# HGRN's level work as instruction threads of its own, and three output-projection blocks beside the last RWKV step

## The reference, cut to what matters

```
# HGRN, each head, forward and backward in time; f = gate in (0,1)
bcum  = cumsum(log f)                       # within a chunk
S     = exp(total) * S + k * exp(total - bcum) @ v
o_t   = sum_{s<=t} (q_t . exp(bcum_t - bcum_s) . k_s) v_s + (q_t * exp(bcum_t)) @ S

# RWKV-7, then the projection of all mixers' outputs
state = state * d + (state @ a) b + v k     # per token
y     = group_norm(state @ r) * ln_w + ln_b + bonus, times g
x     = x + concat(out_a, out_b, out_m) @ w_out
```

## Time and profile before

| what | value |
|---|---|
| time of three runs | 3525.97, 3529.41, 3529.43 us (median 3529.41) |
| the profiled execution | 3524.7 us, of it span 3522.9 us |
| granted TensorE clock, mean | 0.979 of full |
| TensorE busy (PE) | 3341.1 us, 95% |
| VectorE, ScalarE, GpSimd busy | 1490.8, 1082.6, 395.9 us |

### The profile page before, as it was taken

How to read it: one execution, slowest core, us unless ns; L and a number is a source line. 1 busy time by engine, 2 the same in 40 slices (tenths; PEclk the granted TensorE clock), 3 DMA queues, 4 the chain that set the end, 5 groups by cost and what they waited for, 6 DMA issues and landing times. The chain is left out here.

```text
span 3522.9 us, 38396 instructions
## 1 busy us (share of the span) xinstructions
PE 3341.1 (95%) x16568; PEld 2582.1 (73%) x16568; DVE 1490.8 (42%) x2056; ACT 1082.6 (31%) x1619; POOL 395.9 (11%) x386
## 2 busy tenths in 40 slices
PE   6999999889899999999999989999998999999999
PEld 2466666666758888888877766788886888888887
DVE  6256624665444111113346442556543433333333
ACT  4243324334233111112135553233323322222211
POOL 1022202343212000000012000111211100000000
PEclk9999999999999999999999999899998999999999
DMA  5111110000042111112122010000003111110211
GB/s 234 41 60 61 72 39 24 13 13 24 1 153 75 48 48 48 48 36 91 46 72 83 36 37 18 8 1 1 1 1 150 54 48 48 48 48 30 96 44 71
DMA packets 35257, 182.33 MB, mean 52 GB/s; under 512 B 4261, under 2 KB 4261, under 8 KB 21648
## 3 DMA queue, kind: packets, MB, share of 16 engines
q1 hardware_dynamic: 22176, 133.18, 10.6%
q0 software_dynamic: 12912, 46.69, 3.4%
HBM read 161.89 MB, written 17.96 MB: 51 GB/s over the span
## 5 line engine op out<-in xcount | busy, mean ns | idle before, releaser
L537 PE MATMUL ps<-r,r 128*128 128x512 f32 x2656 | 1056.7, 398 | 14.4 <-DVE r L2022 13.2
L538 PE MATMUL ps<-r,r 128*128 128x512 f32 x2656 | 1048.0, 395 | 0.0
L539 PE MATMUL ps<-r,r 128*128 128x512 f32 x2656 | 1047.9, 395 | 0.0
L537 PEld LDWEIGHTS ps<-r,r 128*128 128x128 f32 x2656 | 501.4, 189 | 142.1 <-issue 20.7
L538 PEld LDWEIGHTS ps<-r,r 128*128 128x128 f32 x2656 | 501.7, 189 | 117.2 <-issue 3.0
L539 PEld LDWEIGHTS ps<-r,r 128*128 128x128 f32 x2656 | 501.4, 189 | 115.7
L1407 ACT ACTIVATE ar<-ps 128x512 f32<-128x512 f32 (+3 forms) x330 | 170.1, 541 | 628.1 <-PE ps L1214 119.5
L1369 ACT ACTIVATE r<-ar 128x1024 fp32r<-128x1024 f32 (+1 forms) x170 | 174.4, 1032 | 550.6 <-PE ps L539 510.6
L2015 DVE TENSOR_TENSOR r<-ar,r 128x1024 fp32r<-128x1024 f32 (+1 forms) x170 | 203.8, 1199 | 324.1 <-ACT r L1369 324.0
L527 PE MATMUL ps<-ar 128*128 128x128 f32 (+5 forms) x1844 | 278.0, 314 | 6.4 <-ACT ar L1407 3.3
L527 PEld LDWEIGHTS ps<-ar 128*128 128x128 f32 (+2 forms) x1844 | 218.9, 174 | 57.1 <-issue 31.8
(11 more groups left out here) (286 smaller groups left out, 3561.4 us busy)
## 6 DMA issues: line engine op xcount, KB each, us to landing
ar<-in_w_mod SPq DMA_DIRECT2D x24, 1024.0 KB, 4.8
ar<-in_w_gu SPq DMA_DIRECT2D x22, 1024.0 KB, 4.8
ar<-in_w_up SPq DMA_DIRECT2D x22, 1024.0 KB, 4.8
ar<-in_w_in SPq DMA_DIRECT2D x19, 1024.0 KB, 4.8
ar<-in_w_dn SPq DMA_DIRECT2D x32, 512.0 KB, 3.4
x<-ar POOLq DMA_DIRECT2D x48, 256.0 KB, 2.3
ar<-x POOLq DMA_DIRECT2D x24, 512.0 KB, 7.0
ar<-in_xT POOLq DMA_DIRECT2D x16, 512.0 KB, 13.7
```

Of the source, the lines that this page charges most:

```text
L537: M.matmul(o, whk, hi[k][:, a:a + n], start=k == 0, stop=False)
L538: M.matmul(o, whk, lo_[k][:, a:a + n], start=False, stop=False)
L539: ins = M.matmul(o, wlk, hi[k][:, a:a + n], start=False, stop=k == nk - 1)
```

## The change

Two edits. In HGRN, ScalarE's and VectorE's thread `direction` is cut into `inputs` and `levels`, each padded with empty turns so that every instruction stays in its turn; in each turn both directions' levels now come before both directions' inputs. On VectorE, `level_done(lv - 1)` moves ahead of level `lv`'s multiply. TensorE's and GpSimd's programs for HGRN stay as they are.

At the end of RWKV, fifteen of the sixteen rounded halves move into the turns of step 5 (`rounded_early`, where `prepare` has nothing left to do), and the first three blocks of the output projection (`AHEAD = 3`, half `a = 0`) are issued beside `finish(5)`, four matmuls a turn from the second turn on, with weights split beside them. The homes of `w_out`'s parts are renumbered for the second block so that weights 0 and 1 go to space that is already free. GpSimd loads the residual tiles once the last masks of step 5 are copied and `("mix", 4)` is given, and no longer behind the barrier. The barrier itself stays; behind it ScalarE rounds the sixteenth half and splits weight 3.

```diff
+    HOME_OF = {1: range(7), 2: (1, 2, 0, 3, 4, 5, 6)}
...
+    EARLY = [(k, a) for a in (0, 512) for k in (1, 2, 0, 6, 3, 4, 7)] + [(5, 0)]
+    AHEAD = 3
...
         def out_projection(tag):                                  # TensorE
             for a in (0, 512):
-                for m in range(8):
+                for m in range(AHEAD if tag == 2 and a == 0 else 0, 8):
...
+            def first_blocks():                                   # TensorE
+                yield
+                for m in range(AHEAD):
+                    name = ("wo", 2, m)
+                    key = (*name, 0)
+                    pe.wait_ge(*v_lo.at(("w", name)))
+                    o = claim(key, m, (v_res, key))
+                    wh_, wl_ = homes[split_home[name]]
+                    n_ = 0
+                    for k in range(8):
+                        if m == 0:
+                            pe.wait_ge(*v_lo.at((("mix", 2), (k, 0))))
+                        for w_, x in ((wh_, hhi), (wh_, mlo), (wl_, hhi)):
+                            ins = M.matmul(o, w_[:, k * 128:k * 128 + 128], x[k][:, 0:512], start=n_ == 0, stop=n_ == 23)
+                            n_ += 1
+                            if n_ % 4 == 0 and n_ < 24:
+                                yield
+                    ins.then_inc(*product(key))
+                    yield
...
-            together(finish(5))
+            together(finish(5), first_blocks())
             stage_done(pe, ("pe", "rwkv", 0))
...
-            together(heads(0), heads(1), feed())                  # ScalarE and VectorE
+            together(heads(0, levels), heads(1, levels), heads(0, inputs), heads(1, inputs), feed())
...
         def out_projection(tag, shift):                           # ScalarE
             if tag == 2:
-                split(("wo", 2, 0))
-                for a in (0, 512):
-                    for k in range(8):
-                        mixed(2, k, a)
-                    if a == 0:
-                        split(("wo", 2, 1))
-            for m in range(2, 8):
+                mixed(2, 5, 512)
+            for m in range(2 if tag == 1 else AHEAD, 8):
                 split(("wo", tag, m))
...
+            def first_blocks():                                   # ScalarE
+                split(("wo", 2, 0))
+                split(("wo", 2, 1))
+                for _ in range(9):
+                    yield
+                act.wait_ge(*product.at(("ry", 5)))
+                split(("wo", 2, 2))
...
+            def levels(hh, d):                                    # VectorE
+                for _ in range(12):
+                    yield
+                for lv in range(1, 8):
+                    L, fs, fq = level_block(d, lv)
+                    xq = blk((t1s, Xs)[lv % 2][d], L)[:, :, fq, :]
+                    if lv > 1:
+                        level_done(hh, d, lv - 1)
+                    dve.wait_ge(*a_gate.at(("x", hh, d, lv)))
+                    V.tensor_tensor(xq, xq, blk(qs[hh % 2], L)[:, :, fq, :], ALU.mult).then_inc(*v_gate(("x", hh, d, lv)))
+                    yield
+                    yield
+                level_done(hh, d, 7)
...
             if tag == 2:                                          # VectorE
-                split(("wo", 2, 0))
-                for a in (0, 512):
-                    for k in range(8):
-                        mixed(2, k, a)
-                    if a == 0:
-                        split(("wo", 2, 1))
+                split(("wo", 2, 3))
+                mixed(2, 5, 512)
...
+            def first_blocks():                                   # VectorE
+                yield
+                split(("wo", 2, 0))
+                yield
+                yield
+                split(("wo", 2, 1))
+                for _ in range(8):
+                    yield
+                split(("wo", 2, 2))
...
-        stage_over(pool, "rwkv", 0)                               # GpSimd
+        for j in range(2):
+            pool.wait_ge(*v_evac.at(("rk", (5, j))))
+        pool.wait_ge(*v_step.at(("mix", 4)))
```

More of the change, by code:

```diff
@@ L257, in fetch_ffn @@
             for j in range(2):
-                split(("gu", tag, m, j), ("gu", tag, m), 1024 * j, home=("out", 0) if m == 1 and j == 0 else None)
+                split(("gu", tag, m, j), ("gu", tag, m), 1024 * j, home=("out", HOME_OF[tag][0]) if m == 1 and j == 0 else None)
         for part in range(3):
@@ L1557, in gate_log, with inputs @@
                 A.activation(t1s[d], t1s[d], ACT.Ln, bias=v("one")).then_inc(*a_step(("ln", hh, d)))
-            def direction(hh, d):
+            def inputs(hh, d):
                 z, t1b, kk, kt, ktT = zs[hh % 2][d], t1s[d], kks[d], gs[d], t1s[d]
@@ L1588, in direction @@
                     yield
+                for _ in range(15):
+                    yield
+                if hh < 3:
+                    gate_exp(hh + 1, d)
                 yield
                 yield
+                if hh < 3:
+                    gate_log(hh + 1, d)
+                yield
+            def levels(hh, d):
+                for _ in range(12):
+                    yield
                 for lv in range(1, 8):
@@ L1595, in direction, with heads @@
                     yield
-                    if lv == 7 and hh < 3:
-                        gate_exp(hh + 1, d)
                     yield
                 yield
-                if hh < 3:
-                    gate_log(hh + 1, d)
                 yield
-            def heads(d):
+            def heads(d, part):
                 for _ in range(15 * d):
@@ L1607, in heads @@
                 for hh in range(4):
-                    yield from direction(hh, d)
+                    yield from part(hh, d)
             for part in parts_of(0)[:5]:
                 block(0, *part)
-            together(heads(0), heads(1), feed())
+            together(heads(0, levels), heads(1, levels), heads(0, inputs), heads(1, inputs), feed())
         def mixed(tag, k, a):
@@ L2264, in direction @@
                 ins.then_inc(*v_state(("s", hh, d)))
[L2265 to L2272 removed]
+                for _ in range(16):
                     yield
[L2274 to L2276 removed]
                 if d:
```

80 lines of the change are left out of this document (45 added, 35 removed).

## The result

The changed kernel takes 3496.64 us (median of 4 runs, 3491.95 to 3500.96), the kernel before 3529.42 us beside it. The ratio is 0.9913, with a 95% interval of 0.9898 to 0.9928: 32.8 us faster, where 23 were forecast. The time lies inside the range of 3495 to 3519, near its low end. The profiled execution of the changed kernel took 3495.15 us, against 3524.7 before. The two terms of the sum, 6.5 and 16.5, came out as about 23 and 9.

What follows compares the result with a forecast made beforehand. TensorE was taken to bound the kernel, busy 3341.1 of 3522.9 us, so only idle time and low clock could be won. HGRN's 6.5 plus the tail's 16.5 made 23.0, from 3529.4 to 3506 us; range 3495 to 3519.

Steps and rivals of the forecast that it cites:

- the tail's 16.5: End of RWKV: early projection blocks win 17.9 us if the clock stays up, less 1.4 for a likely fall: 16.5.
- signs of being wrong: Wrong if 0.50 clock outlasts the first block, ScalarE waits for `w_out` beyond 2655, or HGRN's end moves under 3 or over 12 us.
- HGRN, 6.5 forecast: HGRN: 3.5 us from copies before the multiply plus 3.0 from direction 1's levels going ahead of direction 0's inputs.
- the gap itself unchanged in length: HGRN, large gap at 792.38: stays 3.58 us long, with 0.65 us won in all since the start.
- no net change of clock: HGRN: the 6.5 us are won without TensorE's clock changing on balance.
- rival C: HGRN's waits go much further; a gap under 3 us spares the clock's fall: 10 to 20 us more, chance 0.12.
- The gaps like 737.81 and 744.73: HGRN, direction 1's levels: gaps of 0.87 and 1.44 us go, less 0.2 left of the second: 2.1 us won.
- The one like 755.21: HGRN, a head's end: the 2.47 us gap splits into 2.1 and 1.4 us, giving 1.1 us back.
- Rival B: Tail: clock stays at half from 2658 through the readout; 3514 to 3520 us with HGRN's 6.5, chance 0.15.
- the lower bound: Tail: with a clock fall, late weights and a second fall at the barrier, only 10.6 us are won.
- A: HGRN gives nothing because VectorE's stalls push the inputs later by what the copies gain: 3513 us, chance 0.18.
- D: Slower: the second masked copy ahead of the multiply becomes the path at every HGRN level: 3550 us, chance 0.03.

Runs made afterwards that it cites:

- HGRN's part: The kernel before with HGRN's part of the change alone, the tail as before: 3504.18 us, ratio 0.9927.
- copy order alone: The kernel before with each HGRN level's multiply issued behind the two masked copies of the level below, old threads kept: 3516.41 us, ratio 0.9966.
- split first: The changed kernel with late residual loads, fourth weight's split in the last step, and VectorE's half of the first weight's split ahead of the state updates: 3493.10 us.
- B: Experiment on the 3.58 us gap, comparing timelines before and with the masked copies first; kernel before with GpSimd also waiting for VectorE's key differences: 3527.75 against 3527.64 us.
- C: Experiments on the tail's gaps; here the changed kernel with GpSimd's residual loads issued only when the second pair of output weights has landed: 3498.91 us.
- the last kernel: Changed kernel with late loads, fourth split moved, VectorE's first split first, roundings behind the normalization, last head's HGRN levels one turn sooner: 3467.81 us, ratio 0.9834.
- threads alone: The kernel before with HGRN's levels ahead of inputs in a turn, but the multiply still ahead of the copies: 3522.05 us, ratio 0.9984.

## Why the prediction was right, and where it was not

The sign and the range held, and the forecast's way of counting gave the right total only within 10 us, because two errors went opposite ways. That is luck as well as method: with the tail's 16.5 us as forecast and HGRN's 22.8 as measured, the time would have been 3490, outside the range. Two of the prediction's own signs of being wrong came true: HGRN's end moved by 980.19 - 959.24 = 21.0 us, more than 12, and ScalarE waited for `w_out` until 2.3 us after the first state product, which is 2656.3 on the scale of the kernel before and beyond 2655.

**HGRN, 6.5 forecast, 22.8 measured.** The step that failed is "the gap itself unchanged in length", and with it "no net change of clock". It took over 1.34 us for the multiply and left the key differences at 2.42, both measured beside GpSimd, and moved them 1.3 us earlier. But a duration measured in contention holds only at its place: half a microsecond earlier against GpSimd, VectorE wins the ports, the two operations take 1.48 and 0.67, and the gap is 3.58 - 1.64 = 1.94. The second part came with the first: in the profiles of the changed kernel and of HGRN's part the clock does not fall in the first three heads, and HGRN's busy time is 9.1 us less. In the third head, that of the rows shown, the idle time fell from 10.5 to 6.7 us, by 3.7 where 1.65 was forecast (1.6 of it is the large gap), and the clock gave another 3.2. It is not a rule that 1.94 us spares the clock: in the first head it fell behind this gap in three kernels (copy order alone, split first, the last one). This was rival C's mechanism, "a gap under 3 us also spares the fall of the clock"; it had 0.12. Its reason was GpSimd's distances starting earlier with each level; the pairs of timelines in B show another, which of the two engines starts first.

The rest of the rows bears the forecast out. The gaps like 737.81 and 744.73 are gone. The one like 755.21 is split, into 1.40 and 1.22 us (2.1 and 1.4 forecast), and the one like 775.75 is 1.21, as forecast. In the last head 4.29, 2.65 and 1.40 us became 3.57, 1.93 and 1.89, the 0.7 won twice and the half microsecond lost of the sum. The waits for the copy were to fall to about 20 us; no level has one, and waits for the multiply took their place.

**The tail, 16.5 forecast, 9.4 measured.** The frame was right: the block behind two state products, the readout at 7.6 us instead of 13.4, the square's wait at 0.51 (0.5), the normalization under the third block, 3.12 us of idle ahead of the fourth (3.2), ended by weight 3's split. Rival B, the clock at half through the readout, did not happen. The sum had 34.7 + 1.4 = 36.1 us from the first state product to the fourth block, and 39.1 were measured. The first block was 0.9 late: the weights were taken as sharing the queues from their issue on, but moved their first packet 3.5 us after it (C). The fall of the clock was charged at 1.4 and cost 1.9: from the first early block to the end of the third it was 31.3 us here and 29.4 in the run with the split first, where the clock held. And these 29.4 were taken as 27.7: full-speed blocks, state products and readout were added up as if each took beside the others what it takes by itself, but four matmuls and a state product took 1.39 us there, where the sum had 1.2. The gap was 0.1 shorter. 0.9 + 0.5 + 1.7 - 0.1 = 3.0.

Outside this piece, the second fall behind the barrier, 2.0, stood only in the lower bound; 1.9 in the step ahead was missing, where the roundings were called hidden in turns in which both engines wait, while one stood in front of the square; so was a later gap of 0.8; and 0.2 is how the kernel before was read (52.6 for 52.4). 3.0 + 2.0 + 1.9 + 0.8 + 0.2 = 7.9, which is the 16.5 - 8.6 of the profile. The lower bound of 10.6 had set 7.3 us for the two falls and the late weight, which cost 4.8, and nothing for the other items.

**The reserve.** A (HGRN gives nothing) and D (slower) are answered by HGRN's part alone, 22.8 us faster. That VectorE's waits at the multiply fell by 76 us is no proof of it, since 64 of them came back as waits ahead of the copy.

## What to carry to other kernels

When two engines share a resource, a duration in the trace belongs to its moment: before moving such an operation, look at who started first and by how much, and cost it both ways. Count a stall together with the clock behind it: here 13.7 us of idle time brought 9.1 of clock with them. And a rest that is right for one pass of a loop may be wrong for its last: the last head alone held 17 us. Where the same code differs by several microseconds between profiles, as in the windowed attention here, read a small edit from its place, and from more than one profile of it.

## What the runs showed of the chip that was not expected

- A start 0.09 us ahead or 0.42 us behind decides which of two engines pays 1 us: VectorE 1.48 and GpSimd 2.75, or 2.42 and 1.50.
- TensorE's clock does not follow the length of one gap. It fell behind 2.36 and 3.58 us, and was down behind 1.75 and 1.51 with 0.33 of work between. Behind 1.94 it held in the changed kernel (16 matmuls at 777.24 in 2.05 us) and fell in the first head of the last kernel (at 584.66 in 3.68); behind 1.93 it fell with the threads alone (at 668.89 in 3.45). Behind a single gap of 3.01 us among the state products it held with the split first (4 matmuls in 1.20 us) and fell in the last kernel, with the same code there (1.89). Behind 2.47 us it fell in one head and held in another of the kernel before (32 matmuls in 5.44 and 3.81 us).
- The same code ran 50 us of windowed attention at 0.76 or 0.97 of the clock, in profiles that are 7 us apart from the first DFT product to the last step.
- A 1 MB fetch issued 2.8 us behind GpSimd's first of 4.2 MB landed after 10.1 us, and after 4.8 with them gone. The two queues moved packet for packet (195 and 197 in 5.2 us), and the fetch, with packets of twice the size, got two thirds of the bytes, but its first packet came only 3.5 us after its issue, and 1.0 with the loads held back.
